# Five experts' rows multiplied in fp32, two column tiles side by side over unsplit weights, in the last third of a two-block network

## The reference

```python
def moe_swiglu(x, w_router, w1, w3, w2):
    ...
    logits = (xf @ w_router).astype(jnp.float32)
    top_vals, top_idx = lax.top_k(logits, TOP_K)
    gates = jax.nn.softmax(top_vals, axis=-1)
    ...
        return (jax.nn.silu(xb @ w1[e]) * (xb @ w3[e])) @ w2[e]
```

## Time and profile before

| | |
|---|---|
| median of 3 runs | 1926.81 us (1926.72 to 1927.54) |
| profiled execution, its own time | 1926.41 us |
| its span | 1924.3 us |
| TensorE busy, share of the span | 1874.9 us, 97% |
| VectorE | 1480.9 us, 77% |
| ScalarE | 1205.3 us, 63% |
| mean granted TensorE clock | 0.996 |
| DMA | 532.97 MB, 277 GB/s over the span |

### The profile page before, as it was taken

How to read it: one execution, slowest core, us unless ns; L and a number is a source line. 1 busy time by engine, 2 the same in 40 slices (tenths; PEclk the granted TensorE clock), 3 DMA queues, 4 the chain that set the end, 5 groups by cost and what they waited for, 6 DMA issues and landing times.

```text
span 1924.3 us, 27731 instructions
## 1 busy us (share of the span) xinstructions
PE 1874.9 (97%) x10485; PEld 1570.1 (82%) x10485; DVE 1480.9 (77%) x1429; ACT 1205.3 (63%) x1299; POOL 190.9 (10%) x134
## 2 busy tenths in 40 slices
PE   9999999999999999999999999899999999999996
PEld 8977897777988999898777888787788888888774
DVE  6867643477766655776798988788989999999897
ACT  7775533454474433446376776678778878878784
POOL 0032020101021400002023000000000000000070
PEclk9999999999999999999999999999999999999998
DMA  6532586514826555482389999999999999999994
GB/s 249 200 110 88 190 300 230 178 61 153 296 91 231 192 195 178 172 277 79 120 351 380 393 379 370 376 367 377 379 379 379 421 381 369 403 380 391 392 424 197
DMA packets 81019, 532.97 MB, mean 277 GB/s; under 512 B 9392, under 2 KB 12720, under 8 KB 20352
## 3 DMA queue, kind: packets, MB, share of 16 engines
q1 hardware_dynamic: 72704, 501.60, 68.3%
q0 software_dynamic: 7584, 28.64, 4.2%
q10 hardware_dynamic: 608, 1.07, 0.2%
HBM read 513.30 MB, written 14.42 MB: 274 GB/s over the span
## 4 chain that ended last, share of the span: by engine, by line
PE 79%; DVE 10%; issue 5%; ACT 3%; DMA 2%; POOL 0%; DVEq 0%; SPq 0%; ACTq 0%
PE bank L791 70%; DVE wrest L3293 3%; PE bank L1628 3%; DMA ring<-in_w_moe 2%; DVE wrest L3046 1%; ACT whi L2373 1%; DVE whi L3293 1%; PE bank L1006 1%; PE bank L1373 1%; DVE wrest L2452 0%; DMA cst<-in_consts 0%; PE bank L1009 0%; PE bank L1180 0%; PE bank L1094 0%; DVE h L3286 0%
## 5 line engine op out<-in xcount | busy, mean ns | idle before, releaser
L3293 DVE TENSOR_TENSOR wrest<-ring,whi 128x2048 fp32r<-128x2048 f32 x186 | 419.8, 2286 | 49.2 <-ACT whi L2373 49.1
L2373 ACT ACTIVATE whi<-ring 128x2048 fp32r<-128x2048 f32 x186 | 351.7, 1913 | 43.9 <-PE bank L791 38.9
L791 PE MATMUL bank<-whi,packed 128*128 128x512 f32 x848 | 284.9, 399 | 11.2 <-DVE arena L3244 5.3
L3046 DVE TENSOR_TENSOR wrest<-ring,whi 128x2048 fp32r<-128x2048 f32 x88 | 203.7, 2358 | 20.6 <-ACT whi L2243 18.8
L791 PEld LDWEIGHTS bank<-whi,packed 128*128 128x128 f32 x848 | 159.1, 189 | 51.5 <-DVE wrest L3293 8.5
L791 PE MATMUL bank<-wrest,packed 128*128 128x512 f32 x496 | 196.1, 395 | 0.0
L791 PE MATMUL bank<-hTh,wrest 128*128 128x256 f32 x608 | 171.2, 282 | 0.0
L2243 ACT ACTIVATE whi<-ring 128x2048 fp32r<-128x2048 f32 x84 | 156.8, 1917 | 21.1 <-DMA ring<-in_w_moe 20.5
L3293 DVE TENSOR_TENSOR whi<-arena,whi 128x2048 fp32r<-128x2048 f32 x62 | 140.3, 2285 | 13.3 <-ACT whi L2373 13.2
L2452 DVE TENSOR_TENSOR wrest<-ring,fhi 128x2048 fp32r<-128x2048 f32 x33 | 76.5, 2317 | 82.0 <-ACT fhi L1820 81.9
L791 PE MATMUL bank<-whi,hidP 128*128 128x512 f32 x344 | 120.3, 404 | 9.5 <-DVE wrest L3293 5.3
(11 more groups left out here) (562 smaller groups left out, 4665.7 us busy)
## 6 DMA issues: line engine op xcount, KB each, us to landing
ring<-in_w_moe SPq DMA_DIRECT2D x274, 1024.0 KB, 7.6
ring<-in_w_dense SPq DMA_DIRECT2D x135, 1024.0 KB, 4.9
arena<-in_w_moe SPq DMA_DIRECT2D x62, 1024.0 KB, 8.2
row<-in_rows POOLq DMA_DIRECT2D x17, 512.0 KB, 5.1
xg_rows<-ncR POOLq DMA_DIRECT2D x10, 512.0 KB, 21.7
arena<-arena SPq DMA_DIRECT2D x32, 106.5 KB, 4.2
arena<-in_tbias POOLq DMA_DIRECT2D x2, 1536.0 KB, 9.0
y_rows<-ncR POOLq DMA_DIRECT2D x5, 512.0 KB, 39.5
```

What stands on the lines that cost most here:

```text
L791: ins = pe.matmul(out_, lhsT, rhs, start=start, stop=stop, **more)
L2373: S["w_hi"].on(a.activation(whi[:, m % LATE_HI, :], late_raw(m), ACT.Copy))
L3046: S["w_lo"].on(v.tensor_tensor(wrest[:, s, :], ring[:, s, :], whi[:, n % HI_SLOTS, :].bitcast(F32), ALU.subtract))
L3293: S["w_lo"].on(v.tensor_tensor(late_rest(m), late_raw(m), whi[:, m % LATE_HI, :].bitcast(F32), ALU.subtract))
```

## The change

The small lists and the big expert's 64 rows are no longer split. Their rows stay whole in fp32 (`pair_x`, two lists of 64 rows in one tile of 128), and so do the weights: `whole_halves` makes two fp32 matmuls for a k tile, each with the list's 64 rows as stationary operand and one half of the chunk's columns as moving operand; the first writes partitions 0 to 63 of a bank, the second partitions 64 to 127, so they stand in two column tiles of 64. There is nothing to fold: w1's product lies in columns 0 to 255 of bank 0 and w3's in 256 to 511, silu and gate make `hid_small` (128 x 256), and `turn_small` turns it with two transposes. Only big chunks (`SPLIT`) are rounded and rested, through `whi` alone, two chunks ahead of their use (b = m + 2). The first four late chunks (`AHEAD`) come split from the loop before; for them `halves_product` takes both parts one after the other. The big expert's outputs add up in banks 1, 3 and 7 over all seven steps and are copied once (`keep_big`). The big chunks stand one or two places elsewhere, the loads of the packed lists' rows are issued earlier, and the adding of gathered rows (`Y_AT`) stands at earlier m. The core of the diff:

```diff
-EMBED_AT, Y_AT = (4, 8, 12, 15, 18, 21), (244, 247, 251, 251)
-PAIR_LOADED, PAIR_TURNED, CHOSEN_AT, LAST_TURNED = (20, 112), (34, 129), 140, 160
+EMBED_AT, Y_AT = (4, 8, 12, 15, 18, 21), (238, 241, 244, 247)
+PAIR_LOADED, CHOSEN_AT = (8, 90), 130
...
-    places = {1 if k == 1 else k * 21 // 4 for k in range(len(big))}
+    places = {k if k < 2 else 6 + (k - 2) * 21 // 4 for k in range(len(big))}
...
+TURN_AT = [AT["small", t, 3] + 1 for t in range(SMALL_STEPS)]
+BIG_TURN_AT = [AT["big", d, 3] + 2 for d in range(E_STEPS)]
+PAIR_TURNED = [AT["big", d, 4] + 1 for d in (0, 3)]
+LAST_TURNED = AT["big", 4, 4] + 1
+SPLIT = list(range(AHEAD)) + [m for m in range(AHEAD, LAST + 1) if ORDER[m][0] == "big"]
+SPLIT_NO = {m: n for n, m in enumerate(SPLIT)}
...
+        def hi_place(m):
+
+            return m if m < AHEAD else 2 * ((SPLIT_NO[m] - AHEAD) % 2)
+
+        def late_hi(m):
+
+            return whi[:, hi_place(m), :]
+
+        def hi_free(m):
+
+            n = SPLIT_NO[m] - AHEAD
+            return SPLIT[AHEAD + n - 2] + 1 if n > 1 else 2 * n + 2
+
         def late_rest(m):
 
-            s = late_place(m)
-            return wrest[:, s, :] if s < RING else whi[:, s - LATE_RING + HI_SLOTS, :]
+            return wrest[:, late_place(m), :] if m < AHEAD else whi[:, hi_place(m) + 1, :]
...
-            def pair_product(out_, both, w, start, stop):
-
-                mm(out_, both, w[0], start=start, stop=False, skip_group_check=True)
-                return mm(out_, both, w[1], start=False, stop=stop, skip_group_check=True)
...
+            def late_whole(m, k):
+
+                wait_late(pe, m, mids)
+                return late_raw(m).rearrange("p (k n) -> p k n", k=k)
...
+            def list_x(n, kk):
+
+                return pair_x[n // 2][:, kk, half_columns(n % 2, HALF)]
+
+            def whole_halves(out_, x, w, width, start, stop):
 
                 for n in range(2):
-                    for b in range(4):
-                        ins = pe.matmul(ps[bank][:, 256 * n + HALF * b:256 * n + HALF * b + HALF],
-                                        parts[n][:, b * P:(b + 1) * P], fold_ones, start=True, stop=True, skip_group_check=True)
-                S[done].on(ins)
+                    ins = mm(out_[HALF * n:HALF * n + HALF, :], x, w[:, half_columns(n, width)], start=start, stop=stop,
+                             skip_group_check=True)
+                return ins
+
+            def halves_product(m, out_, x, w, k, width, start, stop):
+
+                if m >= AHEAD:
+                    return whole_halves(out_, x, w[:, k, :], width, start, stop)
+                whole_halves(out_, x, w[0][:, k, :].bitcast(F32), width, start, False)
+                return whole_halves(out_, x, w[1][:, k, :].bitcast(F32), width, False, stop)
...
+                w = late_split(m, 4) if m < AHEAD else late_whole(m, 4)
+                if t == 0 and c == 0:
+                    wait(pe, "p_xv", 1)
                 for k in range(4):
                     kk = 4 * (c % 2) + k
-                    ins = pair_product(ps[c // 2][:, :], x[:, kk, :], (wh[:, k, :], wr[:, k, :]), kk == 0, kk == KT - 1)
+                    ins = halves_product(m, ps[0][:, half_columns(c // 2, SEQ)], list_x(1 + l, kk), w, k, SEQ,
+                                         kk == 0, kk == KT - 1)
                 chunks_used.on(ins)
+
+            def turn_small(t):
+
+                wait(pe, "s_hid", t + 1)
+                for b in range(2):
+                    ins = pe.transpose(ps[0][:, b * P:(b + 1) * P], hid_small[:, b * P:(b + 1) * P], ident)
+                S["s_tr"].on(ins)
...
+                w = late_whole(m, 2)
                 for k in range(2):
-                    b = 2 * half + k
-                    for c in range(2):
-                        cs = slice(c * 512, (c + 1) * 512)
-                        ins = pair_product(ps[2 + c][:, :], both[:, b, :], (wh[:, k, cs], wr[:, k, cs]),
-                                           j == 0 and b == 0, j == E_STEPS - 1 and b == 3)
+                    ins = whole_halves(ps[2][:, :], hT_small[t % 2][:, k, half_columns(half, HALF)], w[:, k, :], 512,
+                                       j == 0 and half == 0 and k == 0, j == E_STEPS - 1 and half == 1 and k == 1)
                 chunks_used.on(ins)
...
-                        split_product(ps[4 + c][:, :], (hidE[0][:, b, :], hidR[0][:, b, :]), (wh[:, k, cs], wr[:, k, cs]),
-                                      b == 0, b == 3)
+                        cs = half_columns(c, 512)
+                        split_product(ps[1 + 2 * c][:, :], (hidE[0][:, 2 * half + k, :], hidR[0][:, 2 * half + k, :]),
+                                      (wh[:, k, cs], wr[:, k, cs]), first and k == 0, last and k == 1)
...
-            for m in range(AHEAD, LAST + 1):
-                wait_late(a, m, mids)
-                a.wait_ge(chunks_used.sem, mids * E_CHUNKS + (N_DENSE + m - LATE_HI + 1))
-                S["w_hi"].on(a.activation(whi[:, m % LATE_HI, :], late_raw(m), ACT.Copy))
...
+                b = m + 2
+                if b in SPLIT_NO and b >= AHEAD:
+                    wait_late(a, b, mids)
+                    a.wait_ge(chunks_used.sem, mids * E_CHUNKS + (N_DENSE + hi_free(b)))
+                    S["w_hi"].on(a.activation(late_hi(b), late_raw(b), ACT.Copy))
...
-                S["s_lo"].on(v.tensor_tensor(hidP[t % 2][:, :, HALF:P], hidT.rearrange("p (b n) -> p b n", b=4),
-                                             hidP[t % 2][:, :, 0:HALF].bitcast(F32), ALU.subtract))
...
-                    part, bank = y_big[n][:, 512 * c:512 * c + 512], ps[4 + 2 * n + c][:, :]
-                    S["b_y"].on(v.tensor_tensor(part, part, bank, ALU.add) if d else v.tensor_copy(part, bank))
+                    S["b_y"].on(v.tensor_copy(y_big[:, 512 * c:512 * c + 512], ps[1 + 2 * c][:, :]))
+                S["b_whole"].on(v.tensor_copy(y_64, ps[7][:, :]))
```

More of the change, by code:

```diff
@@ L57 @@
 SCATTERED = ZEROED + 16 * 4
-Y_STORES = 1 + (N_SMALL - 1) + 2
+Y_STORES = 1 + 2 * (N_SMALL - 1) + 3
 HI_SLOTS = 6
@@ L1739, in turn_big @@
                 S["b_tr"].on(ins)
+                wait(pe, "b_hid64", d + 1)
+                for b in range(2):
+                    ins = pe.transpose(ps[6][:, b * P:(b + 1) * P], hid_64[:, b * P:(b + 1) * P], ident)
+                S["b_tr64"].on(ins)
             def turn_pair(q):
@@ L2396, in _ @@
[L2396 to L2402 removed]
+                        copy_64(d)
                 for q in range(2):
[L2404 removed]
+                    if m == PAIR_TURNED[q] + 1:
@@ L3294, in _ @@
+            for m in range(LAST + 1):
                 if m == AHEAD:
                     copy_outputs(mids)
+                for t in range(SMALL_STEPS):
+                    if m == AT["small", t, 3] + 1:
+                        gate_small(t)
                 for d in range(E_STEPS):
-                    if m == AT["big", d, 3] + 3:
+                    if m == AT["big", d, 3] + 1:
                         gate_big(d)
-                    if m == BIG_FOLD_AT[d] + 3:
+                        gate_64(d)
+                    if m == BIG_TURN_AT[d] + 1:
@@ L3329, in _ @@
+                if m == AT["big", E_STEPS - 1, 5] + 1:
+                    keep_big()
+                b = m + 2
+                if b in SPLIT_NO and b >= AHEAD:
+                    wait(v, "w_hi", mids * E_CHUNKS + (MOE_ROUNDED + SPLIT_NO[b] + 1))
+                    S["w_lo"].on(v.tensor_tensor(late_rest(b), late_raw(b), late_hi(b).bitcast(F32), ALU.subtract))
                 if m == CHOSEN_AT:
```

314 lines of the change are left out of this document (102 added, 212 removed).

## The result

| | before | changed |
|---|---|---|
| median of five runs each | 1926.72 us (1925.01 to 1927.54) | 1875.82 us (1873.73 to 1876.14) |
| profiled execution, its own time | 1926.41 us | 1873.73 us |
| its span | 1924.3 us | 1871.8 us |
| TensorE busy | 1874.9 us, 97% | 1800.9 us, 96% |
| VectorE | 1480.9 us, 77% | 989.1 us, 53% |

The changed kernel takes 0.973 of the time of the kernel before (95% interval 0.9717 to 0.9744), 51 us less. I had said 1870 us, range 1857 to 1899.

What follows compares the result with a forecast made beforehand. TensorE bounds the kernel before; transfers become the bound. Landing at 1850 plus 1.8, 0.7 and 14.5 gives a span of 1867 us, 1869 with 2.1 outside; forecast 1870 us, range 1857 to 1899.

Steps and rivals of the forecast that it cites:

- TensorE led before, with the transfers close behind: Late section before the change: TensorE busy 97%, VectorE 90%, DMA share 0.98 at 388 GB/s; TensorE leads, transfers next.
- Two tiles side by side: Small fp32 products in two column tiles of 64 overlap: 0.109 us a record, 1.75 us a chunk.
- the third rival: Small products' tiles of 64 not side by side: time 2260 us, or 2124 with only weight loads paid; chance 6%.
- TensorE's sum: TensorE's late chunks: 1233 us, then 567 of chunks, turns and entries, 20 of split waits; end at 1820 us.
- Splits: Rounding and resting 40 big chunks on ScalarE and VectorE: 4.2 us a split, 20 us of TensorE waits in all.
- The transfers as the bound: Late chunk loads: full stream from 1235 us, 258.2 MB in 615 us, last landing 1850, 30 us after TensorE's sum.
- The size of the rate: Late transfers run at 420 GB/s, taken from the longest fast stretch, 60 us, instead of the mean of 388.
- The end: After the last landing: 1.8 us of matmuls, 0.7 for the output's copy, then 14.5 as before.
- Gathers: Before m = 238: taken as not longer than the earlier 62 us from store to last gather's issue; nothing counted.
- Waits of TensorE as the bound: Splits, turns and copies delay TensorE: 100 us of waits give about 1919 us, half of that 1880; chance 15%.
- Transfers at 388: Late transfers stay at the mean of 388 GB/s: 258.2 MB last 665 us, time 1920 us; chance 8%.
- A falling clock: Last 41 chunks run at 1.2 GHz instead of 2.4, ending up to 41 us later: 1880 to 1911 us; chance 6%.

Runs made afterwards that it cites:

- the last experiment: Changed kernel with nine slots, chunks m = 2 and 3 whole, later big chunks, and identity matmuls between the last sum's halves: 1865.29 us, 0.9681 of the kernel before.

## Why the prediction was right, and where it was 6 us off

**TensorE led before, with the transfers close behind: right, with VectorE closer than I said.** With one eighth of the folds left, 32 of 64 us came, and then VectorE stood at 95%. My reading of TensorE's time was off, though: of the 691 us I called 656 work and 35 waits, mostly for splits. The trace has 19 us of waits after 1219.0, 11.7 of them for splits, so the work was 672 us.

**Two tiles side by side: shown.** 0.108 us a record (0.109 predicted), and 2270 us with one tile (2260). The Trainium skill (TensorE: Matmul & The Clock Gate, Part 3) would let a load overlap only with a matmul of another row group; by that the third rival's 2124 us would have come. The trace disagrees: records of the same row group stand 0.108 us apart with a load for each (on the page 2032 loads for the 2032 matmul records on raw ring slots).

**TensorE's sum: 10 us low.** I had its end at 1820; with fewer bytes it is 1829.6, with 17 us of waits (20 predicted). The work of its 248 chunks and turns is thus 580 us and not 567. Some 5 of these 13 us are in the big chunks: twelve split matmuls take 3.00 us up to the next start (1248.57 to 1251.57), where I had counted 2.78 and 0.1 for the entry; that is 0.12 x 40 = 5 us. The rest was not traced; a shortfall of 16 us (672 less 656) lay in the sum for the kernel before too. Behind 1290 us it lay under the transfers and cost nothing.

**Splits: right.** 13.9 us of TensorE's waits for them, in 15 times. Trading these for waits at the turns gained nothing; raising them to 71.5 cost nothing.

**The transfers as the bound: right, but not from 1235 on.** This is the step that failed, though the mechanism behind it held. I had a full stream from 1235, with chunk 12, because TensorE leaves its four dear chunks there. But at that moment many of the slots hold landed chunks and TensorE is behind. It catches up slowly, since its mean chunk (580 / 248 = 2.34 us) is not much shorter than a transfer (2.47), and here come two of the dear chunks, three big ones and a wait of 1.3 us for a split: by TensorE's timeline the fifteen chunks m = 2 to 16 are used up from 1225.3 to 1267.8, 2.83 us each. The rate from 1235 to 1290 was 380 instead of 420: (420 - 380) x 55 / 420 = 5.2 us. The experiments show it twice over: with less work in the first four chunks the stretch has 420 and the time is 7 us less; with small chunks first it has 424, where the same kernel without that order has 404.

**The size of the rate: 422 where I took 420.** Over 560 us that gives 2.7 us back. That the two misses had opposite signs is luck. The bytes, 262.6 MB where 263.0 were before, were nearly right: 6.7 MB beside the chunks, where I carried over 6.5 and the earlier trace rows give 7.1. 5.2 less 2.7 is 2.5 us; the last landing came at 1853.2 us, 3.2 after the 1850 predicted.

**The end: 1.6 us low.** From the last landing to the end of the span 18.6 us, 17.0 predicted. I carried over the 14.5 us from the kernel before and missed that the diff puts the identity matmuls ahead of both halves of the last sum: 5.05 us from the last chunk's start to VectorE's addition against 4.03 with them between the halves. Of the 1.6 us this is 1.0, read from the last experiment's trace.

**Gathers: hidden, and far shorter.** From the store of the last small list but one to the last gather's end 25 us went by, not 62 (rows below).

**The sum of the misses.** 3.2 us of landing, 1.6 of tail: span 1871.8 instead of 1867. The profiled execution lay 2.1 us under the median, where the one before lay 0.3 to 0.4 under its own; the other 1 us or so of the 5.8 between 1870 and 1875.8 is that choice of execution and rounding.

**The rivals.** Waits of TensorE as the bound: no (13.9 us for splits, and 26 us of room). The times given for this rival don't agree with each other: waits of 100 us do give 1919, but half of them end the chunks at 1850 and give 1870, not 1880. Nor do eight slots of 2.5 us less two under way give 13 us of cover, but 15. Transfers at 388: no, 422. A falling clock: the page's slices stay at 9, and in the tail (1850 to 1871) it was 0.80; where an experiment brought it to 0.78 beside full transfers, it cost nothing, in an engine that had that time to spare. **The sign I would not name again:** SyncE's wait for TensorE "far under 533 us". It was 486.

Where the change's larger saving went: it took the end of TensorE's own work on the chunks from 1909.8 to 1829.6, 80 us, and the transfers let 55 of these through, to 1855.2.

## What to carry to other kernels

When TensorE and the transfers are both near full, work out both ends apart and find the point at which the one hands over to the other: until then the stream runs at TensorE's pace, and a few us of dear chunks at the start cost their full price, while the same us later cost nothing. Read the rate by stretches beside the queue's waits; a queue with a fixed number of slots reports waits for its consumer whichever of the two is late. The stream can be full long before the engine waits for a load: here from 1290 us on, while TensorE's first wait for one came at 1777. At the end, put what the critical engine needs last behind what the next engine needs first, and don't look for a hole in a loop whose holes are shorter than the work.

## What the runs showed of the hardware

**Transfers to one core at 422 GB/s for 560 us** (share 1.01), and the same 421 to 422 with less matmul work, nine slots or other places of the big chunks. The Trainium skill (DMA: Bandwidth & Descriptors, Specifications) has about 358 GB/s as a core's limit, and I had set the traces against it. The same page (Bandwidth) says that 358 is what each of two cores gets when both stream, and has 425 GB/s for one core alone. This kernel runs on one core, and its 422, over a stretch nine times as long as the 60 us seen before, agrees with that second figure.

**fp32 in two column tiles of 64** runs two tiles in the time of one, the same 64 rows stationary in both and another half of the chunk moving past each: 0.108 us a record of 256 columns, against 0.22 with both products in one tile.

**GpSimd's indirect transfers were issued in 1.0 us each here, not in 9 to 14.** GpSimd's timeline of the changed kernel, which answers to the earlier trace rows:

```profile
1762.57 1.12 POOL L762 DMA_DIRECT2D y_rows<-arena  x2 [126.78 <-DVE arena L3226]
...
1782.58 1.02 POOL L776 DMA_INDIRECT arena<-y_rows,from_i  x1 [10.02 <-DMA y_rows<-h]
1783.90 0.98 POOL L776 DMA_INDIRECT arena<-y_rows,from_i  x1 [0.30 <-issue]
...
1786.42 0.94 POOL L776 DMA_INDIRECT arena<-y_rows,from_i  x1 [0.31 <-issue]
```

Before, three of the four took 8.8, 13.5 and 11.3 us, with VectorE busy 44.8 of 45 us around them (1830 to 1875), and the kernel with fewer folds, in which VectorE was busy 67.6 of 70 us, the same (9.2, 13.5, 11.3). Here VectorE is busy 0.4 of 10 us (1780 to 1790), and they take 0.9 to 1.0; so too in the kernel with one tile. The transfers stood at 424 and 415 GB/s around the long issues, at 422 and 364 around the short ones. So a busy VectorE and long issues go together here, and the rate of the transfers doesn't tell them apart; that the one causes the other was not tested by itself.
